# Expert blocks of 32 rows in four column groups, turned by VectorE

## The reference

```python
    def expert_block(args):
        x_b, e = args
        hid = jax.nn.silu(x_b @ w_gate[e]) * (x_b @ w_up[e])
        return hid @ w_down[e]
...
    return jnp.einsum('tkd,tk->td', y_assign, gates.astype(h.dtype))
```

## Time and profile before

| | |
|---|---|
| median of 3 runs | 865.18 us (863.8 to 866.1) |
| profiled execution, span | 864.3 us |
| its own time beside the span | not listed; the median lies 0.9 us above the span |
| TensorE busy | 831.4 us (96%) |
| VectorE, ScalarE, GpSimd busy | 418.5, 215.9, 140.0 us |
| moved by DMA | 261.95 MB, 303 GB/s over the span |
| chain that ended last | TensorE 81%, VectorE 12%, DMA 3% |

### The profile page before, as it was taken

One profiled execution on the slowest core, in us unless ns is written; L12 is line 12 of the kernel. 1 busy time (PEld: TensorE's weight loads), 2 busy tenths in 40 slices (PEclk: granted clock), 3 DMA queues, 4 the chain that ended last, 5 costly groups with the idle time before them and its releaser, 6 DMA issues.

```text
span 864.3 us, 15988 instructions
## 1 busy us (share of the span) xinstructions
PE 831.4 (96%) x5906; PEld 563.8 (65%) x5907; DVE 418.5 (48%) x825; ACT 215.9 (25%) x461; POOL 140.0 (16%) x279
## 2 busy tenths in 40 slices
PE   7999999999999999799999999999999999999995
PEld 5888988777877888665555555555555555555541
DVE  4699999986564535563222222222222222222237
ACT  3423211557875333101110011110111101111013
POOL 3300010000000011112222212222122222122101
PEclk9999999999999999899999999999999999999999
DMA  7353645131253198889999999999999999999998
GB/s 198 79 137 101 184 180 178 58 87 36 75 166 128 69 412 314 349 345 406 420 417 418 377 405 419 417 421 418 420 418 420 422 419 420 420 419 421 419 387 322
DMA packets 81143, 261.95 MB, mean 303 GB/s; under 512 B 19274, under 2 KB 45130, under 8 KB 56523
## 3 DMA queue, kind: packets, MB, share of 16 engines
q1 hardware_dynamic: 63392, 240.92, 71.3%
q0 software_dynamic: 7888, 18.78, 5.6%
q10 hardware_dynamic: 9818, 1.66, 1.0%
HBM read 246.49 MB, written 24.20 MB: 313 GB/s over the span
## 4 chain that ended last, share of the span: by engine, by line
PE 81%; DVE 12%; DMA 3%; issue 2%; SPq 1%; ACT 1%; POOL 0%; POOLq 0%; DVEq 0%; ACTq 0%
PE ps L1490 30%; PE ps L1536 16%; PE ps L1214 9%; PE ps L1350 8%; DVE big L1968 7%; PE ps L1504 3%; PE ps L1428 3%; PE ps L1266 2%; PE ps L1233 2%; DMA big<-results 2%; PE ps L1245 1%; PE ps L1493 1%; DVE w_split L1905 1%; DMA big<-h_rows,idx_of 1%; PE ps L1173 1%
## 5 line engine op out<-in xcount | busy, mean ns | idle before, releaser
L1493 PE MATMUL ps<-ring,big 128*64 128x256 f32 x688 | 153.9, 382 | 0.2 <-DMA ring<-in_w_up 0.2
L1490 PE MATMUL ps<-ring,big 128*64 128x256 f32 x672 | 150.3, 382 | 1.2 <-issue 1.2
L1214 PE MATMUL ps<-hT,w_split 128*128 128x256 f32 (+1 forms) x744 | 136.9, 341 | 0.0
L1490 PEld LDWEIGHTS ps<-ring,big 128*64 128x64 f32 x672 | 92.5, 138 | 56.7 <-issue 13.5
L1830 ACT ACTIVATE big<-ps 64x256 f32<-64x256 f32 x78 | 29.3, 376 | 392.5 <-PE ps L1493 341.6
L1214 PEld LDWEIGHTS ps<-hT,w_split 128*128 128x128 f32 x744 | 113.5, 190 | 20.5 <-issue 7.0
L2301 DVE TENSOR_TENSOR big<-ps,big 64x256 f32<-64x256 f32 x78 | 33.2, 426 | 182.5 <-ACT big L1830 155.1
L1490 PE MATMUL ps<-big 128*64 128x256 f32 x544 | 120.2, 379 | 0.0
L1493 PE MATMUL ps<-big 128*64 128x256 f32 x544 | 120.2, 379 | 0.0
L1490 PEld LDWEIGHTS ps<-big 128*64 128x64 f32 x544 | 74.5, 137 | 46.5 <-issue 9.7
L1493 PEld LDWEIGHTS ps<-ring,big 128*64 128x64 f32 x688 | 94.7, 138 | 1.7 <-DMA ring<-in_w_up 0.7
(11 more groups left out here) (298 smaller groups left out, 1197.4 us busy)
## 6 DMA issues: line engine op xcount, KB each, us to landing
ring<-in_w_down SPq DMA_DIRECT2D x44, 1024.0 KB
ring<-in_w_up SPq DMA_DIRECT2D x43, 1024.0 KB, 15.1
ring<-in_w_gate SPq DMA_DIRECT2D x42, 1024.0 KB
big<-in_w_gate SPq DMA_DIRECT2D x20, 1024.0 KB, 7.2
big<-in_w_up SPq DMA_DIRECT2D x20, 1024.0 KB
big<-in_w_down SPq DMA_DIRECT2D x20, 1024.0 KB
w_raw<-in_w_in SPq DMA_DIRECT2D x20, 512.0 KB, 3.8
results<-spare POOLq DMA_DIRECT2D x12, 512.0 KB, 3.3
```

Source lines behind the costliest of these rows:

```text
L1214: mm = pe.matmul(ps[:, n % 2, 0:size], w_split[:, sub, hi_w, k, :], hT[:, k // 4, hi_h, k % 4, cols], **flags)
L1490: pe.matmul(ps[0:BLK, 6 * h, 0:FH], xT[:, k, q, :], gate[2][:, k, fs], **flags)
L1493: mm = pe.matmul(ps[BLK:2 * BLK, 6 * h + 1, 0:FH], xT[:, k, q, :], up[2][:, k, fs], **flags)
```

## The change

Blocks have 32 rows (`BLK = 32`), and a row is cut into quarters (`QS = 4`), so that 32 rows fill 128 partitions with 256 elements each. Gate/up runs in four column groups of 32 columns, with 128 moving columns each: two for gate and two for up. Down runs in four groups with 256 moving columns. The stationary operands are `xT` (128 x 32 for each of 8 pieces of the contraction) and `hbT` (128 x 32 for each of 4).

The turning is done by VectorE with its transposition inside 32 partitions: `take_rows` turns the gathered quarter rows into `xr`, `rows_in` multiplies them by the norm's weight into `xT`, `hidden_half` turns each half of the inner activations into `hbT`. `turn_rows` and `turn_hidden` are gone, and with them ScalarE's two copies. For this the weights' rows are dealt to partitions as p*8+k over the whole matrix, not over each half; a load is still 128 pieces of 8 KB. The landing buffer is freed by `residual` (`base_ready`), not by a copy. TensorE counts its blocks in a register, and reads the number of blocks of the next expert before each down product.

The row indices, now for 62 blocks, are summed in four column groups and added up with one matmul more each (`sums_of_rows`, `rows_and_gates`); `sums_of_rows` stands inside block 0, before its down product. Near the end the quarters of the last block's rows are put in order by two scaled copies (`late_rows`).

```diff
-BLK = 64
+BLK = 32
+QS = P // BLK
 MAXB = 2 * T // BLK + E
...
+        xb2 = [next_of_block(QD) for q in range(2)]
+        xT = next_of_block(KD * BLK).rearrange("p (k n) -> p k n", k=KD)
...
-        xb = spare[:, 0:HD]
+        xr = spare[:, 0:QD].rearrange("p (k n) -> p k n", k=KD)
...
             def weights_of(e, w, ks):
-                return w[0, bass.ds(e, 1), ks.start * P:ks.stop * P, :].rearrange("e (p k) d -> p (e k) d", p=P)
+                return w[0, bass.ds(e, 1)].rearrange("e (p k) d -> p (e k) d", p=P)[:, ks, :]
...
                     store_rows(2 * i + q, q)
                     scales_column(2 * i + (q + 2), q)
-                    pool.wait_ge(xb_copied, 2 * i + (q + 3))
+                    pool.wait_ge(base_ready, 2 * i + (q + 3))
                     load_rows(2 * i + (q + 4), q)
...
             def gate_up(gate, up, q, h):
 
-                fs = slice(h * FH, (h + 1) * FH)
                 for k in range(KD // 2):
                     flags = dict(start=(q == 0 and k == 0), stop=(q == 1 and k == KD // 2 - 1))
-                    if h == 0 and k == 0:
-                        pe.wait_ge(gate[0], gate[1])
-                    pe.matmul(ps[0:BLK, 6 * h, 0:FH], xT[:, k, q, :], gate[2][:, k, fs], **flags)
-                    if h == 0 and k == 0:
-                        pe.wait_ge(up[0], up[1])
-                    mm = pe.matmul(ps[BLK:2 * BLK, 6 * h + 1, 0:FH], xT[:, k, q, :], up[2][:, k, fs], **flags)
+                    for a, (landed, target, w) in enumerate((gate, up)):
+                        if h == 0 and k == 0:
+                            pe.wait_ge(landed, target)
+                        for c in range(2):
+                            at, f = (2 * a + c) * BLK, (2 * h + c) * P
+                            mm = pe.matmul(ps[at:at + BLK, 6 * h, 0:P], xT[:, q * KD // 2 + k, :], w[:, k, f:f + P], **flags)
...
+            def expert_block(s, target, halves, following, first=False):
+                b = pe.snap(at_block, min_val=0, max_val=MAXB - 1)
                 pe.wait_ge(xt_ready, b + 1)
                 for q in range(2):
                     for h in range(2):
                         gate_up(*halves[q], q, h)
-                turn_hidden(b, 0)
-                pe.wait_ge(xb_copied, b + 2)
-                pe.sem_inc(pe_passed, 1)
-                turn_rows()
-                turn_hidden(b, 1)
+                if first:
+                    sums_of_rows()
+                    pe.wait_ge(table_ready, 2)
+                pe.reg_mov(count, pe.value_load(table[0:1, bass.ds(following, 1)], min_val=1, max_val=MAXN))
                 pe.wait_ge(y_evac, b + 1)
+                pe.wait_ge(dn_in[s][0], target)
+                pe.wait_ge(dn_in[s][1], target)
+                pe.wait_ge(ht_ready[0], b + 1)
+                pe.wait_ge(ht_ready[1], b + 1)
                 for k in range(KF):
-                    if k % (KF // 2) == 0:
-                        pe.wait_ge(ht_ready[k // (KF // 2)], b + 1)
-                        pe.wait_ge(dn_in[s][k // (KF // 2)], target)
-                    pe.matmul(ps[0:BLK, 2, :], hbT[:, k, :], down_w[s][:, k, 0:512], start=(k == 0), stop=(k == KF - 1))
-                    mm = pe.matmul(ps[BLK:2 * BLK, 2, :], hbT[:, k, :], down_w[s][:, k, 512:1024],
-                                   start=(k == 0), stop=(k == KF - 1))
+                    for c in range(QS):
+                        mm = pe.matmul(ps[c * BLK:(c + 1) * BLK, 2, 0:QD], hbT[:, k, :], down_w[s][:, k, c * QD:(c + 1) * QD],
+                                       start=(k == 0), stop=(k == KF - 1))
                 mm.then_inc(y_done, 1)
...
                     act.wait_ge(gu_done[h], b + 1)
-                    nc.scalar.activation(sG[:, h * FH:(h + 1) * FH], ps[0:BLK, 6 * h, 0:FH], ACT.Silu).then_inc(sg_ready[h], 1)
-                act.wait_ge(ht_ps[0], b + 1)
-                nc.scalar.activation(hbT[:, 0:KF // 2, :].rearrange("p k n -> p (k n)"), ps[:, 5, 0:KF // 2 * BLK],
-                                     ACT.Copy).then_inc(ht_ready[0], 1)
...
+                    nc.scalar.activation(sG[h * 2 * BLK:(h + 1) * 2 * BLK], ps[0:2 * BLK, 6 * h, 0:P], ACT.Silu).then_inc(sg_ready[h], 1)
...
+            def take_rows(b, q, landed):
+                dve.wait_ge(xb_in[q], 16 * landed)
+                dve.wait_ge(xt_ready, b)
+                nc.vector.transpose(out=xr, in_=xb2[q].rearrange("p (n k) -> p k n", k=KD)).then_inc(xb_turned, 1)
...
             def rows_in(b):
-                dve.wait_ge(xt_ps, b + 1)
-                nc.vector.tensor_tensor(xT, ps[:, 4, :].rearrange("p (k s n) -> p k s n", k=KD // 2, s=2),
...
+                dve.wait_ge(xb_turned, b + 1)
+                dve.wait_ge(gu_done[1], b)
+                nc.vector.tensor_tensor(xT, xr, n2_T[:].unsqueeze(2).to_broadcast([P, KD, BLK]), ALU.mult).then_inc(xt_ready, 1)
...
             def hidden_half(b, h):
...
-                nc.vector.tensor_tensor(hb[:, fs], ps[BLK:2 * BLK, 6 * h + 1, 0:FH], sG[:, fs],
-                                        ALU.mult).then_inc(hb_ready[h], 1)
+                nc.vector.tensor_tensor(hb[own], ps[2 * BLK:4 * BLK, 6 * h, 0:P], sG[own], ALU.mult).then_inc(hb_ready[h], 1)
+                dve.wait_ge(hb_ready[h], b + 1)
+                nc.vector.transpose(out=hbT[own], in_=hb[own].rearrange("p (n k) -> p k n", k=KF)).then_inc(ht_ready[h], 1)
...
             def expert_block(b, q, stored, rows, next_q, landed):
-                hidden(b)
+                hidden_half(b, 0)
+                residual(b + 1, 1 - q, rows, b + 1)
+                hidden_half(b, 1)
                 rows_in(b + 1)
                 result(b, q, stored)
-                residual(b + 1, after)
-                copy_rows(b + 2, next_q, landed)
+                take_rows(b + 2, next_q, landed)
```

More of the change, by code:

```diff
@@ L566, in encoder @@
         br, n2_column, lg = next_of_once(NR), next_of_once(KD), next_of_once(NT * NR).rearrange("p (t n) -> p t n", t=NT)
-        base = once[:, 0:HD]
-        n2_T = sb("n2_T", [P, 2, KD // 2])
+        base = [once[:, q * (QD + 2 * NB):q * (QD + 2 * NB) + QD] for q in range(2)]
+        n2_T = sb("n2_T", [P, KD])
         ident = sb("ident", [P, P])
@@ L1127, in _ @@
             scales_column(2 * pairs + 4, 0)
[L1128 removed]
+            pool.wait_ge(xb_kept, 2)
             load_rows(2 * pairs + 5, 0)
@@ new lines, in expert_block, with blocks, expert @@
+                mm.then_inc(y_done, 1)
+                pe.reg_add(at_block, at_block, 1)
+            def blocks(s, target, halves, following):
+                pe.reg_mov(number, count)
+                with pe.Fori(0, pe.snap(number, min_val=1, max_val=MAXN)):
+                    expert_block(s, target, halves, following)
+            def expert(place, s, target, head, following=None):
+                blocks(s, target, in_slot(s, target, head), place + 1 if following is None else following)
@@ L1577, in late @@
                 for half in range(2):
-                    own = slice(half * BLK, (half + 1) * BLK)
-                    mm = pe.matmul(ps[:, LATE_BANK[t] + half, :], late_hot[own, t, :], yb2[1][own, :], start=True, stop=last)
+                    own = slice(half * P // 2, (half + 1) * P // 2)
+                    mm = pe.matmul(ps[:, LATE_BANK[t] + half, :], late_hot[own, t, :], late_rows[own, :], start=True, stop=last)
                 return mm
@@ new lines, in _ @@
+                residual(b + 1, 0, xb2[1], b + 2)
+                take_rows(b + 2, 0, pairs + j + 4)
+                keep_rows(b + 2)
+            last = 2 * pairs + rest + 4
+            hidden_half(last - 1, 0)
+            hidden_half(last - 1, 1)
+            rows_in(last)
+            result(last - 1, 0, pairs + rest + 1)
+            link(V.tensor_scalar(odd_quarter[:], quarter_of[:], -3.0, None, ALU.is_equal))
+            link(V.scalar_tensor_tensor(odd_quarter[:], quarter_of[:], -1.0, odd_quarter[:], ALU.is_equal, ALU.add))
```

297 lines of the change are left out of this document (153 added, 144 removed).

## The result

| | before | with the change |
|---|---|---|
| median | 865.22 us (4 runs, 863.8 to 866.1) | 893.48 us (4 runs, 889.61 to 895.82) |
| ratio | | 1.032, 95% interval 1.0295 to 1.0346 |
| span of the profiled execution | 864.3 us | 894.0 us |

The change costs 28 us; 863.2 with 876 as the upper end was forecast. The profiled execution with the change was the slowest of its four (895.82 us), which is why its span lies above the median; the spans differ by 29.7 us, the medians by 28.3. The page answers to the earlier trace rows with these lines: the DMA digit of 380 to 402 us is 6, and from there on it drops to 8 again and again, TensorE is no longer full, and the queues moved the same bytes in no more packets.

What follows compares the result with a forecast made beforehand. TensorE and the weight stream were both taken as full, the stream setting the span: -4.9 + 2.8 + 0.4 + 1.5 - 1.8 = -2.0, span 862.3, median 863.2 us; range 858 to 876.

Steps and rivals of the forecast that it cites:

- What bounds the kernel: From 500 to 780 us TensorE and the DMA weight stream are both full; 16.0 us of stream an expert.
- The edge and its price: In the long experts the stream stays full up to 7.05 us a block; each 0.1 us beyond costs 4.5 us.
- TensorE's new block: Gate/up 3.49, chain to down 1.30, down 1.73, 0.1 for branches: 6.7 us used, bounds 6.4 to 7.4, against 11.94.
- The bound for issue: Gate/up's upper bound: 64 matmuls issued at 0.058 us a pair of 64-column matmuls take 3.74 us.
- All bounds together: Upper bounds of gate/up, chain, down and branches (3.74, 1.7, 1.73, 0.2): a 7.4 us block, 878 us span.
- All this costs nothing while the block is over 6 us: GpSimd's 4.5 us round, gathers some 10 us ahead and VectorE's 2.6 us a block fit inside TensorE's block.
- The new pause at 387: Weight stream: six loads end at 387 us, the next is asked for near 387.8, data 2 us later: +2.8 us.
- Rival 2: Waiting for weights drops TensorE to 1.2 GHz, slowing long experts entered cold and the end: +3 to +10 us, chance 0.13.
- Rival 1: TensorE becomes the bound, by upper bounds (7.4 us a block) or poor packing (7.8, +34 us): mostly 869 to 880, chance 0.20.
- Pauses that go: Stream pauses at 370 to 380 us, at 380 and at 490 to 500 us vanish: -4.9 us.
- Pieces of 1 KB: Rows travel in 1 KB pieces, not 2, 6144 pieces more at 8 ns fixed if each is a packet: +1.5 us.
- The end: The result read-back queues directly behind the last weights, so only its landing stays: -1.8 us.

Runs made afterwards that it cites:

- run 2: On top of run 1, gate/up in 32 matmuls of 256 moving columns instead of 64 of 128, one transposition before down: 874.91 us, ratio 1.0099.
- run 5: Kernel with the change, but GpSimd issues a block's scatter only after the next block's gate/up: 873.07 us, ratio 1.0097.
- run 7: On top of run 2, a few filler matmuls of 512 columns on constants (1, 4, 2 and 2) in TensorE's early waits: 870.19 us, ratio 1.0064.
- run 3: Kernel with the change plus 17 matmuls of 512 columns on constants, ahead of block 0 and between its gate/up and block 1: 899.7 us.
- run 6: On top of run 5, a few filler matmuls of 512 columns on constants (1, 4, 2 and 2) in TensorE's early waits: 873.56 us.
- run 4: Kernel with the change, but down in 32 matmuls of 128 moving columns instead of 16 of 256: 917.69 us.
- run 1: Kernel with the change, but VectorE forms the next block's residual behind rows_in again, not between the activation halves: 892.34 us.
- run 9: On top of run 5, the gather issued right behind the scatter, its indices copied before the scatter: 888.02 us.

## Why the prediction was wrong, point by point

- **What bounds the kernel** held in the main. Where TensorE was slower than 7.05 us a block the stream lost 24 us, and with blocks of 7.0 to 7.2 us (runs 2 and 5) only 5 in the same window. ("No pause from 400 us on" was misread, as its own window of 490 to 500 us has a share of 0.81; and the stretch from block 0's start to the end of the last block is 473 us, from 366.0 to 839.1, not 39 x 11.94 = 466, since block 0 took 18.4.) The edge and its price were right in kind and a little low: 0.45 to 0.5 us over it cost 24 us in the long experts, where 4.5 a tenth gives 20 to 22. The DMA share alone tells too little of it: from 500 to 780 us it fell by 0.06, 17 us, and the bytes by 24 us' worth.
- **The step that failed is "TensorE's new block"**, in its terms for gate/up and the chain. Counted as there (a term ends where the next pass would have started), gate/up took 3.97 us (4.18 less 0.21 of tail) where 3.49 was taken and 3.74 was the bound, and the chain to down 1.84 where 1.30 was taken and 1.7 was the bound; down took 1.73 (725.36 to 727.08), as forecast. The step of 0.109 us with four groups was right. What was put at nothing is the hole of gate/up beside GpSimd's indirect DMA, 0.48 us, and what it does to the chain: the first half's silu came 0.57 us ahead of the second's, not 0.87, so the residual was not done in time and held the second product up by 0.42 us. The bound for issue was taken from 48 records in a stretch without GpSimd work. The transposition lay inside its bounds, 0.40 for 0.29. With the scatter out of the way (run 5) the block was 7.0 to 7.2 us and 20 of the 28 us were back.
- **The range.** All bounds together gave 7.4 us a block and a span of 878, a median of about 879, but the range was closed at 876. The block of 7.5 us lies above its bound as well.
- **"All this costs nothing while the block is over 6 us"**, said of GpSimd, was the wrong question. GpSimd had time for its round; what its indirect DMAs do to TensorE was not looked for, and in the kernel before it could not be seen, since the passes of 0.216 us a step ran through the gather of the earlier trace rows evenly. Its other half, that a gather starts some 10 us before VectorE takes the rows, failed at block 2: 6.9 us in the kernel with the change (378.49 to 385.36), and VectorE waited 2.50 us for it.
- **The new pause at 387** was named but mis-sized, 2.8 for 8.6 us. The next load was asked for at 394.71 instead of 387.8. Block 0 to block 1 took 15.1 us for 13.9, and block 1 took 11.6 for 6.7, with its clock at half for most of it (TensorE's timeline, SyncE's, and a window). The clock is the smaller part of the miss: with TensorE's waits filled the pause was still 6.2 us (run 7), against 9.3 without (run 2, 208 GB/s from 380 to 400 us). VectorE's wait for the gather, told there, is one cause of what is left; the rest is not taken apart.

```profile
380.97 5.98 PE L1509 MATMUL ps<-ring,big 128*32 128x128 f32 x128
389.22 3.54 PE L1545 MATMUL ps<-ring,big 128*32 128x256 f32 x32 [2.27 <-DVE big L2316]
```
```profile
394.71 0.34 SPq L863 DMA_DIRECT2D ring<-in_w_gate  x1
```
```profile
390.00:392.00 2.00, 2.00 (x24) 1.12 (x20) 0.00 (x0) 0.00 (x0) 1.14 (x2) 0.50 0.00 0
```

- **Rival 2, the clock**, had the right mechanism, but for the most part at another place: at block 1, after the waits of 372 to 380 us. Experiments 3, 6 and 7 show it: with these waits filled, block 1's gate/up takes 3.70 or 3.66 us. Among the long experts two blocks were hit, those begun at 560.44 and 772.16 (8.88 and 8.96 us for 7.5), where up to 5 us for an expert was forecast.
- **Rival 1** is what happened, TensorE became the bound, but by neither of its prices (7.4 and 7.8 us a block; 7.5 was measured). The rule of the Trainium skill weighed there (TensorE: Matmul & The Clock Gate, three column groups giving 2.38) does not hold here: four groups side by side kept the step of 0.109 us, and 0.216 with 256 columns. That the time came out near what that rule would give (+34 us) is chance: the block has 7.5 us for another reason.
- **The smaller terms.** Pauses that go: -4.9 forecast, -5.0 measured by the windows. Pieces of 1 KB: +1.5 forecast, nothing measured; GpSimd's queue had 7632 packets and 18.79 MB against 7888 and 18.78. The end: the reads were issued at 862.43, ahead of the last weights (landed 837.85 + 28.88 = 866.73) as forecast; from the last weight piece to the end it took 27.7 us (866.3 to 894.0) against 28.8 (835.5 to 864.3), -1.1 for -1.8. The mean time of an 8 KB piece was 323 ns with the change against 318 before, and 319 in run 7, where the pauses of the long experts are gone; between 520 and 540 us, with the stream full in both, it was 315 in run 7 and 315 before. So the new order of the weights' rows cost nothing that can be seen.

SyncE's issue of the reads, with the change:

```profile
862.43 6.86 SPq L979 DMA_DIRECT2D big<-results  x12
```

## What to carry to other kernels

Before matmuls are made shorter to fill the array with column groups, count them and look at what GpSimd issues beside them: the same columns in half as many matmuls, or the scatter a few microseconds later, were worth 18 to 20 us here. In these kernels the hole came in nearly every block where matmuls of 128 columns ran at full clock beside an indirect DMA from its start to its end. When a resource is nearly full on two sides, the last tenths of a block cost a multiple of what the others cost (4.5 us a tenth here), so a block's cost needs an upper bound taken from a stretch where the other engines are at work. A wait of some microseconds ahead of an urgent stretch is worth filling with matmuls that end just before it; too many of them cost more than the clock gives.

## What the runs showed of the hardware that was not expected

- While GpSimd issues an indirect DMA of 128 descriptors (1.01 to 1.07 us in the blocks), TensorE can run dry, which is to say that its passes stop though nothing that the profile shows holds them: holes of 0.2 to 0.6 us with matmuls of 128 columns, in gate/up and in run 4 in down too, and none with 256 columns (gate/up in runs 2 and 7, down in the kernel with the change). There is none in blocks 0 and 1 of runs 3 and 6, whose gate/up was over before an indirect DMA had run for 0.9 us beside it. And there is none in block 1 of the kernel with the change, where a gather (384.04 to 385.07) lies wholly inside a gate/up at half clock: 128 columns again, but taken half as fast. The hole went or moved with the indirect DMA in runs 1, 5 and 9. A memset of 0.52 us did not bring it, but was too short to tell.
- That it is the delivery of instructions which fails is the reading that fits, since the hole depends on how fast TensorE takes its matmuls; no view shows it, and a shared path that delays something else is not excluded. The Trainium skill, Runtime: NRT & Kernel Launch, "Instruction fetch mechanics", says that a taken branch whose target is not among the loaded instructions forces a fetch before execution goes on. That is not what happens here: in the kernel with the change the two instruction queues moved nothing between 478.2 and 826.6 us, there is no hole at the branch between blocks, and the holes lie 21 to 117 passes behind it.
- The hole's place in the records is not exact. Silu of the first half waits for the 96th pass, which by the records began at 729.64, ahead of the hole; it started at 730.73, 0.8 us later than the wait behind a last pass usually lasts (about 0.3 us). So the 0.8 to 1.0 us after which a hole begins is by the records alone. In run 9 the result of the block before (L2337, 656.43) was late in the same way. What is certain is that TensorE as a whole was late by the hole.
- VectorE's transposition inside 32 partitions took 0.40 us for 64x128 and also for 128x128 (run 2), and 0.65 for 128x256: 1.95 ns for each further element of a partition, where the product has 1.05.
